# Loading all experts' weights four tiles at a time, in runs of 32 KB, in a fused two-block kernel

## The reference

```python
def moe_expert_choice(h, router_w, w_gate, w_up, w_down):
    cap = CAPACITY_FACTOR * T // N_EXPERTS            # 32 tokens per expert
    aff = jax.nn.softmax((h @ router_w), axis=-1)
    gate, idx = lax.top_k(jnp.swapaxes(aff, 1, 2), cap)
    xs = h[bidx, idx]
    hid = silu(einsum('becd,edf->becf', xs, w_gate)) * einsum('becd,edf->becf', xs, w_up)
    ye = einsum('becf,efd->becd', hid, w_down) * gate[..., None]
    return zeros_like(h).at[bidx, idx].add(ye)
```

## Time and profile before

| | us |
|---|---|
| median of 3 runs (1550.35 to 1550.72) | 1550.49 |
| the profiled execution | 1551.3 |
| its span | 1549.5 |
| TensorE busy | 1207.3 |
| VectorE busy | 562.5 |
| ScalarE busy | 423.9 |
| bytes moved by DMA | 520.9 MB |

### The profile page before, as it was taken

One profiled execution on the slowest core, in us unless ns is written; L12 is line 12 of the kernel. 1 busy time (PEld: TensorE's weight loads), 2 busy tenths in 40 slices (PEclk: granted clock), 3 DMA queues, 4 the chain that ended last, 5 costly groups with the idle time before them and its releaser, 6 DMA issues.

```text
span 1549.5 us, 18615 instructions
## 1 busy us (share of the span) xinstructions
PE 1207.3 (78%) x8122; PEld 730.7 (47%) x8122; DVE 562.5 (36%) x829; ACT 423.9 (27%) x553; POOL 29.9 (2%) x36
## 2 busy tenths in 40 slices
PE   4999999999656656656666656656666899999998
PEld 1878899943111212111111111211211589999997
DVE  3887776511101101101101101101101497777566
ACT  2865646232000000000000000000000454467545
POOL 0012000000000000000000000000000000000000
PEclk9999999999778878778867888878778999999999
DMA  9546859699999999999999999999999855555551
GB/s 364 207 156 229 301 209 337 223 403 429 426 428 428 428 428 427 428 428 426 428 428 427 427 428 428 427 427 429 428 427 428 327 164 163 163 183 184 184 186 55
DMA packets 118719, 520.90 MB, mean 336 GB/s; under 512 B 7264, under 2 KB 85088, under 8 KB 90736
## 3 DMA queue, kind: packets, MB, share of 16 engines
q1 hardware_dynamic: 118496, 519.64, 83.9%
q10 hardware_dynamic: 144, 0.09, 0.0%
HBM read 518.66 MB, written 1.05 MB: 335 GB/s over the span
## 4 chain that ended last, share of the span: by engine, by line
DMA 53%; PE 43%; DVE 2%; ACT 1%; SPq 1%; issue 0%; DVEq 0%
DMA pair<-in_wu 27%; PE B L1697 16%; DMA pair<-in_wd 12%; DMA pair<-in_wg 11%; PE B L1705 6%; PE B L2113 4%; PE B L1709 3%; DMA wslot<-in_w_in 2%; PE B L1824 2%; PE B L2147 1%; PE B L1675 1%; PE B L1812 1%; PE B L1827 1%; DMA wslot<-in_w_out 1%; DMA wslot<-in_ada_w 1%; PE B L2074 0%
## 5 line engine op out<-in xcount | busy, mean ns | idle before, releaser
L2113 PE MATMUL B<-pair,xs 128*32 128x512 f32 x2048 | 323.1, 758 | 193.0 <-DMA pair<-in_wu 121.5
L2113 PEld LDWEIGHTS B<-pair,xs 128*32 128x32 f32 x2048 | 63.2, 124 | 413.0 <-issue 180.1
L2147 PE MATMUL B<-pair,hidT 128*32 128x512 f32 x1008 | 167.9, 799 | 102.1 <-DMA pair<-in_wd 96.6
L1697 PE MATMUL B<-hnh,whj 128*128 128x256 f32 x488 | 138.1, 283 | 0.0
L1697 PE MATMUL B<-hnh,wslot_r 128*128 128x256 f32 x488 | 137.6, 282 | 0.0
L1697 PE MATMUL B<-hn_r,whj 128*128 128x256 f32 x488 | 137.1, 281 | 0.0
L2147 PEld LDWEIGHTS B<-pair,hidT 128*32 128x32 f32 x1008 | 32.3, 128 | 218.6 <-DMA pair<-in_wd 143.2
L955 DVE TENSOR_TENSOR wslot_r<-wslot,whj 128x2048 fp32r<-128x2048 f32 x52 | 118.9, 2289 | 31.3 <-ACT whj L509 31.3
L509 ACT ACTIVATE whj<-wslot 128x2048 fp32r<-128x2048 f32 x51 | 97.2, 1913 | 87.6 <-PE B L1697 82.0
L1289 DVE SCALAR_TENSOR_TENSOR x<-B,mod,x 128x256 f32<-128x256 f32 x128 | 56.0, 480 | 163.5 <-PE B L2092 163.3
L1320 DVE COPY ye<-B 128x512 f32<-128x512 f32 x15 | 10.4, 692 | 269.6 <-PE B L2147 269.6
(11 more groups left out here) (505 smaller groups left out, 1908.8 us busy)
## 6 DMA issues: line engine op xcount, KB each, us to landing
pair<-in_wg SPq DMA_DIRECT2D x64, 2048.0 KB, 41.2
pair<-in_wu SPq DMA_DIRECT2D x64, 2048.0 KB, 40.9
pair<-in_wd SPq DMA_DIRECT2D x62, 2048.0 KB, 40.9
wslot<-in_w_in SPq DMA_DIRECT2D x58, 1024.0 KB, 5.2
aslot<-in_ada_w SPq DMA_DIRECT2D x20, 1024.0 KB, 7.2
wslot<-in_ada_w SPq DMA_DIRECT2D x4, 1024.0 KB, 9.1
wslot<-in_w_out SPq DMA_DIRECT2D x4, 1024.0 KB, 8.5
wslot<-in_wa SPq DMA_DIRECT2D x4, 1024.0 KB, 5.1
```

The source lines that it names most:

```text
L1697: mm = e.matmul(ps, w[:, k, :], x(k), start=k == 0 and j == 0, stop=k == kn - 1 and j == 2)
L2113: mm = e.matmul(B[b][32 * j:32 * j + 32, :], XS[x // 8][:, k, 32 * (x % 8):32 * (x % 8) + 32], tile_at_page(t)[:, 512 * j:512 * j + 512], ...
L2147: mm = e.matmul(B[3 + db][32 * r:32 * r + 32, :], hidT[:, 128 * c + 32 * j:128 * c + 32 * j + 32], v2(tile_at_page(t + c // 2))[:, c % 2, ...
```

## The change

The loads are listed in `LOADS` as (first tile, number of tiles, page). Tiles 0 to 27 stay pairs in the places that they had, with the parted pair at tiles 18 and 19. From tile 28 to tile 379 four tiles at a time are loaded by one DMA, 88 of them, into four places of four pages in turn: slots 0 to 3, pages 8 to 11, pages 0 to 3, pages 4 to 7. The last two loads are pairs again, tiles 380 and 381 into pages 8 and 9, tiles 382 and 383 into pages 10 and 11 by two DMAs as before. Page 12 is left out, so 16 MiB of places remain instead of 18. A partition now takes four rows of the gate or up matrix (eight of the down matrix), 32 KB in one run. TensorE waits once per load, and SyncE issues a load of four when all tiles that lay in its four pages have been used. Since other features share a partition now, the gather steps by 4, `hid` is turned by sixteen products of 64 x 64 with the identity instead of four transposes, and `ffs` by sixteen instead of four. One buffer of the second block (`whj2`) and `c2` change their pages.

```diff
-        WH2 = [put(f"whj{i}", 2048, page(p), FR) for i, p in enumerate((14, 15, 6))]
+        WH2 = [put(f"whj{i}", 2048, page(p), FR) for i, p in enumerate((14, 15, 0))]
...
-        c2, c2l = both("c2", 2048, page(0))
+        c2, c2l = both("c2", 2048, page(6))
...
-        PAIRS = TURN[:2] + [EXTRA] + TURN[3:] + [APART] + 2 * (TURN[:2] + TURN[3:])
-        PAIRS += [TURN[i % 9] for i in range(12 * NE - len(PAIRS))]
-        tile_page = lambda t: PAIRS[t // 2]
+        LOADS = [(2 * i, 2, r) for i, r in enumerate((zone_at(2), zone_at(4), EXTRA, zone_at(0), zone_at(6), 0, 2, zone_at(8), zone_at(10), APART,
+                                                      zone_at(2), zone_at(4), zone_at(0), zone_at(6)))]
+        for t in range(28, 24 * NE, 4):
+            r = zone_at(8) if t == 24 * NE - 4 else (0, zone_at(8), zone_at(0), zone_at(4))[(t - 28) // 4 % 4]
+            LOADS += [(t, 2, r), (t + 2, 2, r + 2)] if t == 24 * NE - 4 else [(t, 4, r)]
...
+        def before(load):
+
+            t0, n, r = load
+            earlier = [x[0] + x[1] - 1 for x in LOADS if x[0] < t0 and any(in_slot(s, x) for s in range(r, r + n))]
+            return max(earlier) if earlier else None
+
+        def expert_src(t, n):
             e_, m, k = t // 24, t % 24 // 8, t % 8
             if m == 2:
-                return a["wd"][e_, 256 * k:256 * k + 512, :].rearrange("(p c) n -> p (c n)", c=4)
-            return a["wu" if m else "wg"][e_, 128 * k:128 * k + 256, :].rearrange("(p c) n -> p (c n)", c=2)
+                rows = a["wd"][e_, 1024 * (k // 4):1024 * (k // 4) + 1024, :].rearrange("(p c) n -> p (c n)", c=8)
+            else:
+                rows = a["wu" if m else "wg"][e_, 512 * (k // 4):512 * (k // 4) + 512, :].rearrange("(p c) n -> p (c n)", c=4)
+            return rows[:, k % 4 * SLOT:(k % 4 + n) * SLOT]
...
-                elif before(t) is not None:
-                    e.wait_ge(*p_exp.at("tile", before(t)))
-                elif tile_page(t) == zpair(12):
-                    e.wait_ge(*a_moe.at("xs", 1, 7))
+                elif before(load) is not None:
+                    e.wait_ge(*p_exp.at("tile", before(load)))
                 experts(t)
...
-            for b_ in range(2):
-                for hf in range(2):
-                    mm = e.matmul(B[4][64 * hf:64 * hf + 64, 0:16].rearrange("p (m q b) -> p b m q", m=2, b=2)[:, b_], ident[:, b_::2],
-                                  ffs.rearrange("p (m q h) -> p h m q", m=2, h=2)[:, hf], start=True, stop=True)
+            for b_ in range(4):
+                for hf in range(4):
+                    mm = e.matmul(B[4][32 * hf:32 * hf + 32, 0:16].rearrange("p (m q b) -> p b m q", m=2, b=4)[:, b_], ident[:, b_::4],
+                                  ffs.rearrange("p (m q h) -> p h m q", m=2, h=4)[:, hf], start=True, stop=True)
...
-                    if k % 2 == 0:
+                    if t == load_of[t][0]:
                         e.wait_ge(*landed[tile_page(t)].at("expert", t))
...
-                for c in range(4):
-                    mm = e.transpose(B[2][:, half(c)], hid[:, c::4], ident)
+                for c in range(8):
+                    for q in range(2):
+                        mm = e.matmul(B[2][64 * q:64 * q + 64, 64 * c:64 * c + 64].rearrange("p (j s) -> p j s", j=2), hid[:, c::8],
+                                      ident.rearrange("p (j q s) -> p q j s", q=2, s=32)[:, q], start=True, stop=True)
```

More of the change, by code:

```diff
@@ L312, in program @@
-        pairs = {r: put(f"pair{r}", 2 * SLOT, page(17) if r == EXTRA else slots_at + r * SLOT if r < BASE else page(r - BASE)) for r in set(PAIRS) - {APART}}
+        APART = EXTRA + 2
+        LOADS = [(2 * i, 2, r) for i, r in enumerate((zone_at(2), zone_at(4), EXTRA, zone_at(0), zone_at(6), 0, 2, zone_at(8), zone_at(10), APART,
[3 more added lines that the diff above has]
+            LOADS += [(t, 2, r), (t + 2, 2, r + 2)] if t == 24 * NE - 4 else [(t, 4, r)]
@@ L313, in program @@
+        load_of = {t: load for load in LOADS for t in range(load[0], load[0] + load[1])}
+        tile_page = lambda t: load_of[t][2]
+        homes = {(n, r): put(("pair" if n == 2 else "four") + str(r), n * SLOT, page(17) if r == EXTRA else slots_at + r * SLOT if r < BASE else page(r - BASE))
+                 for _, n, r in LOADS if r != APART}
         apart = (slots[4], put("apart", SLOT, page(15)))
         def tile_at_page(t):
-            return apart[t % 2] if tile_page(t) == APART else pairs[tile_page(t)][:, t % 2 * SLOT:t % 2 * SLOT + SLOT]
@@ L318, in program, with last_tile @@
[L318 to L325, removed]
+            t0, n, r = load_of[t]
+            return apart[t - t0] if r == APART else homes[n, r][:, (t - t0) * SLOT:(t - t0 + 1) * SLOT]
+        in_slot = lambda s, load: load[2] <= s < load[2] + load[1]
+        def last_tile(s):
+            return max(load[0] + load[1] - 1 for load in LOADS if in_slot(s, load))
@@ L362, in program @@
             signal(n, 16) for n in ("l_vec", "l_x", "l_ctx", "l_id", "l_msk", "l_iota", "l_wst", "l_bsb", "l_wr", "l_gkw", "l_wgk", "l_wpp", "l_pT", "l_last_down"))
-        landed = [signal(f"landed{i}", 16) for i in range(BASE + MORE + AUX + 2)]
+        landed = [signal(f"landed{i}", 16) for i in range(BASE + MORE + AUX + 3)]
         stored = signal("stored", 16)
@@ L461, in sync @@
                     experts(8)
-            for t in range(10, 24 * NE, 2):
+            for load in LOADS[5:]:
+                t = load[0]
                 if t == 10:
@@ L481, in sync @@
                 if n < SECOND + 4:
-                    e.wait_ge(*p_exp.at("tile", last_tile(tile_slot(n) // 2 * 2)))
+                    e.wait_ge(*p_exp.at("tile", last_tile(tile_slot(n))))
                 elif n == SECOND + 4:
-                    e.wait_ge(*p_exp.at("tile", max(i for i in range(24 * NE) if tile_page(i) == APART)))
+                    e.wait_ge(*p_exp.at("tile", last_tile(APART)))
                 else:
@@ L488, in sync @@
                 if n == SECOND + BASE - 1:
-                    e.wait_ge(*p_exp.at("tile", last_tile(zpair(10))))
+                    e.wait_ge(*p_exp.at("tile", last_tile(zone_at(11))))
                     e.dma_start(wgk[0:16, :], a["w_gk2"]).then_inc(*l_gk())
@@ L720, in scalar @@
                 if k == 7:
-                    e.wait_ge(*p_exp.at("tile", 2 * PAIRS.index(EXTRA) + 1))
+                    e.wait_ge(*p_exp.at("tile", last_tile(EXTRA)))
                     pp_left(0)
```

28 lines of the change are left out of this document (14 added, 14 removed).

## The result

| | before | with the change |
|---|---|---|
| median of 20 runs each, us | 1550.8 (1549.49 to 1551.94) | 1553.64 (1551.05 to 1557.47) |
| profiled execution, us (span) | 1551.3 (1549.5) | 1551.3 (1549.5) |
| forecast | | 1545.9, range 1541.5 to 1553 |

The ratio is 1.0017, with a 95% interval of 1.001 to 1.0023: slower by 2.8 us, where I had forecast 4.6 us less. The profiled execution of the change is among its quicker ones, 2.3 us under its median. What is read from the profiles is therefore set against profiled times, 1551.3 on both sides.

The account below looks back on a forecast made before the run. The prediction took the DMA stream of expert weights as the bound. Its terms, -6.6 + 2.0 + 0 + 0 = -4.6 us, took the profiled 1551.3 to 1546.7; with the median 0.8 lower it forecast 1545.9 us, range 1541.5 to 1553.

Parts of the forecast that it names:

- What bounds the kernel: Experts: the DMA stream of weights bounds them, and TensorE's work is hidden while it keeps ahead of the places needed.
- What a longer run saves: Expert weight stream: 704 fixed packet parts of 9.4 ns go per engine, -6.6 us (0 to -12.4).
- A1: Rival, weight stream: engines cut 32 KB into 16 KB packets again, so nothing is saved; 1552.5 us, 20%.
- A2: Rival, weight stream: only half of the 9.4 ns belongs to a packet, saving 3.3 us; 1549.2 us, 8%.
- C: Rival, weight stream: long runs are carried slower, 1% more per packet giving 1561 us; 6%.
- B: Rival, experts: TensorE becomes the bound if its clock falls to 1.2 GHz, +54 us to 1604; 3%.
- What the start costs: First expert: the first load of four waits for tile 13 where a pair needed tile 11, +2.0 us (0 to 2.8).
- What the small products cost: Router and experts' `hid` turning: more, narrower products on TensorE, covered by waits and idling; 0, up to +0.8 us.
- The step that failed: Gather and reading of `hid`: wider steps counted at nothing, inside TensorE's idling of the steady part.
- Four tiles and the waits: Steady part: fewer places and later releases don't run the queue dry, as TensorE can be 15 us late; 0 us.
- the tail: End of the experts: tiles 376 to 379 land together, work finishing before the next landing; 0, +1.7 us if TensorE is slow.
- The sum: Whole kernel: -6.6 + 2.0 + 0 + 0 = -4.6 us, giving 1545.9 us.

Follow-up runs that it names:

- e7: e3, but each load of four takes two runs of 16 KB per partition instead of one of 32 KB: 1551.43 us, ratio 1.0002.
- e3: The changed kernel with the gather reading 128 neighbours and tiles 28 to 43 loaded as pairs: 1544.6 us, ratio 0.996.
- e1: The changed kernel with ScalarE writing `H2k` so that the gather reads 128 neighbours: 1547.0 us, ratio 0.9975.
- e5: The changed kernel with only half of the sixteen products that turn `hid`: 1551.83 us, ratio 1.0007.
- e9: e1 with VectorE writing `hid` in the order in which the turning reads it: 1547.38 us, ratio 0.9974.
- e4: The kernel before, in pairs, with the gather reading at a step of 4 instead of 2: 1555.48 us, ratio 1.003.
- e8: e3 with VectorE writing `hid` in the order in which the turning reads it, 64 neighbours: 1544.28 us, ratio 0.9955.
- e10: The changed kernel with only `hid` written in the turning's order, the gather still at a step of 4: 1554.85 us, ratio 1.0019.

## Why the prediction was wrong

- **What bounds the kernel**: right for the steady part, and the mean clock was 0.81.
- **What a longer run saves**, -6.6 us: right. The packets became 32.7 KB and the rate 431. e7 against e3 gives 6.4 to 6.8 us for 672 packets per engine, 9.5 to 10.2 ns each (9.1 by the steady windows), where 9.4 was forecast; for the change's 704 packets that is 6.4 to 7.2 us. A1, A2 and C fall with it, and B with the clock.
- **What the start costs**, +2.0: about right for what it meant, the grain beside a quick gather (2.4, e1 against e3). In e1 the first load of four was issued at 340.69 and landed 14.5 us later, where I had 341.11 and 15.0; the second was issued at 350.26, with 4.9 us still to land. In the change both readings fail, since tile 13's use, taken from the trace before, came at 345.20. The load then landed after 12.5 us, at 357.7 instead of 356.1. The 10.1 us that I gave a pair in a nearly empty queue were of an issue with another pair ahead of it (issued at 322.56, landed 11.2 us later); all but alone it took 7.2. "The next load of four waits for tile 17, at about 349, and the queue then holds more than 5 us of work": it came at 356.81, with 0.9 us left.
- **What the small products cost**: 0, and it was 0 at the end. The turning came out at the size forecast (2.2, and 2.16 measured), but by luck: one of its instructions takes 133 ns (16 in 2.13 us, e5), near my upper bound of 145, and the 32 take no longer than 16, since the two passes run side by side. I had neither. Where its cost falls in the first expert it can't be told from nothing (e9 against e1). The router's 32 instructions took 0.66 us where eight took 0.41. Nothing shows harm from that: the experts' first gather product starts at 313.59, and at 314.54 and 313.06 in two profiles with the old form (before, e4).
- **The step that failed** is the sentence "Wider steps in the gather and in reading `hid` I count at nothing, inside the same idling". The idling, 2.0 to 2.9 us ahead of a pair, is that of the steady part. In the first expert there is none: the earlier trace rows had TensorE busy for all 5 us from 332 to 337 at a DMA share of 0.94, and I had written that pairs are issued there one by one as TensorE lets go of tiles. The cover was looked up in one stage and spent in another. It measured +3.4 (under pairs) to +6.6 us (under fours) by the medians, 3.1 and 4.3 by the profiled executions. A sign of the cost stood in the trace of the kernel before: its transposes of `hid` (line 2132) load weights at a step of 4 and took half as long again for it as those of line 2124, which load neighbours. That would have bounded the term instead of leaving it out. Grouped lines, 312 to 392 us:

```profile
L2132 PEld LDWEIGHTS B<-ident,hid 128*128 128x128 f32 x8 | 1.1, 209 | 3.6 <-DVE hid L1309 3.6
L2124 PEld LDWEIGHTS B<-ident,pr 128*128 128x128 f32 x4 | 0.4, 140 | 1.7 <-issue 1.7
```

- **Four tiles and the waits**, 0 in the steady part, and **the tail**, 0 (+1.7 possible): right. The last load of four took 5.15 us, between the 3.8 and the 6.4 that I had weighed, and the two pairs behind it 1.92 each; the second block's start waited for its weights to land and not for them.
- **The sum**: -6.6 + 2.0 = -4.6 was forecast. From the medians of the runs it is -6.4 for the run (e7 to e3), +0.2 for all else that e3's kernel changes (e7 over the kernel before, which is no more than noise), +2.4 for the grain and +6.6 for the gather's step beside it: +2.8. None of my rivals was this case. The one that ended slower by a late TensorE, B, looked at the steady part too.

## What to carry to other kernels

A cost is hidden only if there is idling in the stage where it falls: before a term is set to nothing, take a window of every stage in which the instruction runs, the first pass above all, where buffers are still handed on one by one. When a layout changes for the DMA's sake, follow it to each operand that now reads at a step, and let the engine with time to spare (here ScalarE, once) write it in the order that the busy one reads. Large loads belong where the queue is deep; while it is shallow, the small grain that frees and fills places early is worth more than the long run.

## What the runs showed of the hardware

- A TensorE weight load of 128 x 128 fp32 took 189 ns from neighbouring columns (e1), 196 at a step of 2 (before) and 324 to 325 at a step of 4 (the change, e4); one of 64 columns 138 ns from neighbours (e8) and 217 at a step of 8 (the change). In transposes it was 140 ns from neighbours and 209 at a step of 4 (before). So a step of 2 is almost free, and one of 4 costs 70% in products and 50% in transposes.
- ScalarE's copy of `H2k` took 683 ns in the order before and 682 in e1's, which reads PSUM at a step of 4; VectorE's product with both inputs at a step of 8 took 1068 ns (e8) instead of 688 (e1).
- One packet of 32 KB in place of two of 16 KB saves 9.1 to 10.2 ns on its engine (e7 against e3). The Trainium skill (DMA: Bandwidth & Descriptors, section Why small descriptors are slow) has about 3 cycles per packet, at the 850 MHz of its section Where 436 GB/s comes from an estimate of 3.5 ns; the measurement decides here, and it is nearly three times as much.
- Into a queue that had run dry or all but, a load of 2 MiB landed 7.2 us after its issue (the change) and one of 4 MiB 12.1 (e10) to 12.5 us (the change).
- Eight fp32 products of 64 columns (16 instructions) that write one half of the PSUM partitions took 2.13 us (e5), and sixteen (32) that write both halves in turn 2.16 (the change).
